# The experts of a decoder layer: square and scaling of finished rows later in full blocks, two low parts earlier, the gather ahead of the store

## The reference

```python
def run_block(args):
    xb, e = args
    h = jax.nn.silu(xb @ w_gate[e]) * (xb @ w_up[e])
    return h @ w_down[e]

ys = lax.map(run_block, (xs, block_expert)).reshape(P, D)
out = jnp.zeros((T + 1, D), jnp.float32).at[slot_tok].add(ys.astype(jnp.float32) * slot_gate[:, None])[:T]
```

## Time and profile before

| | us |
|---|---|
| median of three runs | 2077.36 (2075.55 to 2087.81) |
| the profiled execution | 2084.54 |
| its span, first to last instruction | 2082.6 |
| PE busy in the span | 1935.8 (93%) |
| DVE busy | 1344.3 (65%) |
| ACT busy | 1166.8 (56%) |
| POOL busy | 868.4 (42%) |

### The profile page before, as it was taken

The page is one execution under the profiler, slowest core; times in us unless marked ns, Lnnn a source line. Parts: engine busy times, 40 slices in busy tenths (PEclk is TensorE's granted clock), DMA queues, the critical chain, the costliest instruction groups (busy, mean ns, idle before and its releaser), DMA issues. The chain is left out here.

```text
span 2082.6 us, 39849 instructions
## 1 busy us (share of the span) xinstructions
PE 1935.8 (93%) x12329; PEld 1646.0 (79%) x12330; DVE 1344.3 (65%) x2479; ACT 1166.8 (56%) x2436; POOL 868.4 (42%) x1044
## 2 busy tenths in 40 slices
PE   7999999979999999989999679899999999999996
PEld 6888888867777787878878568788888888788885
DVE  5333333339888888845656559766777777787764
ACT  4211111128888889853333248666666667686763
POOL 3332222213656644431332335445454345344544
PEclk9999999979999999989999889999999999999998
DMA  7433334375363543224543569968878978987852
GB/s 224 147 122 122 121 121 123 114 187 151 107 189 98 131 112 92 69 72 152 166 167 126 209 197 368 359 219 295 288 267 289 361 243 292 364 300 288 287 196 71
DMA packets 230803, 406.35 MB, mean 195 GB/s; under 512 B 31201, under 2 KB 169057, under 8 KB 206480
## 3 DMA queue, kind: packets, MB, share of 16 engines
q1 hardware_dynamic: 201328, 352.08, 49.7%
q0 software_dynamic: 29376, 53.03, 9.6%
HBM read 345.83 MB, written 111.15 MB: 219 GB/s over the span
## 5 line engine op out<-in xcount | busy, mean ns | idle before, releaser
L747 ACT ACTIVATE prob<-score,nmax 128x512 f32<-128x512 f32 (+3 forms) x464 | 264.4, 580 | 24.7 <-DVE nmax L897 24.1
L65 PE MATMUL proj<-w_in_lo,n1T_hi 128*128 128x512 f32 (+1 forms) x640 | 242.8, 379 | 3.5 <-DVE w_in_lo L250 3.4
L897 DVE TENSOR_REDUCE nmax<-score 128x2 f32<-128x1024 f32 (+3 forms) x232 | 212.5, 920 | 39.9 <-PE score L945 38.4
L66 PE MATMUL proj<-w_in_hi,n1T_lo 128*128 128x512 f32 (+1 forms) x640 | 237.3, 371 | 0.0
L67 PE MATMUL proj<-w_in_hi,n1T_hi 128*128 128x512 f32 (+1 forms) x640 | 237.1, 371 | 0.0
L812 POOL TENSOR_SCALAR prob<-prob,scale,lam 128x512 f32<-128x512 f32 (+3 forms) x168 | 139.1, 840 | 152.7 <-DVE scale L884 143.1
L1774 POOL DMA_INDIRECT acc_scratch<-y,own x47 | 143.9, 3062 | 96.7 <-ACT y L1955 79.7
L269 DVE TENSOR_TENSOR cosx<-proj,rope_sb 128x512 f32<-128x512 f32 (+1 forms) x64 | 37.9, 592 | 213.2 <-PE proj L67 213.2
L1978 DVE TENSOR_TENSOR wd_lo<-raw_pieces,wd_hi 128x1024 fp32r<-128x1024 f32 x128 | 148.2, 1217 | 7.5 <-ACT wd_hi L1962 7.5
L764 ACT COPY aT<-aT_ps 128x512 f32<-128x512 f32 (+3 forms) x232 | 122.6, 528 | 51.0 <-PE aT_ps L962 49.1
L1978 DVE TENSOR_TENSOR wg_lo<-raw_pieces,wg_hi 128x1024 fp32r<-128x1024 f32 x124 | 146.9, 1218 | 5.3 <-ACT wg_hi L1940 3.9
(11 more groups left out here) (305 smaller groups left out, 5532.9 us busy)
## 6 DMA issues: line engine op xcount, KB each, us to landing
raw_pieces<-in_w_down SPq DMA_DIRECT2D x64, 1024.0 KB, 9.7
raw_pieces<-in_w_gate SPq DMA_DIRECT2D x62, 1024.0 KB, 6.4
raw_pieces<-in_w_up SPq DMA_DIRECT2D x62, 1024.0 KB, 7.6
qk_scratch<-qkT SPq DMA_DIRECT2D x94, 256.0 KB, 2.4
xT_sb<-in_xT SPq DMA_DIRECT2D x16, 512.0 KB, 5.1
h<-in_x SPq DMA_DIRECT2D x16, 512.0 KB, 6.3
acc_scratch<-h SPq DMA_DIRECT2D x16, 512.0 KB, 3.0
n_scratch<-n SPq DMA_DIRECT2D x16, 512.0 KB, 5.5
```

The lines of the kernel that those rows point to most:

```text
L65: pe.matmul(out, hi, w_lo, start=first, stop=False)
L66: pe.matmul(out, lo, w_hi, start=False, stop=False)
L747: act.activation(prob[:, n % RING, c, 0:w], score[:, n % BUFS, c, 0:w], ACT.Exp, bias=nmax[:, c, n:n + 1], accum_out=part[:, c, n:n + 1]). ...
L897: dve.tensor_reduce(nmax[:, :, n:n + 1], score[:, n % BUFS, :, 0:w], AX.X, ALU.max, negate=True).then_inc(max_ready, 1)
```

## The change

In full blocks four things move; nothing is added or taken away, and small blocks stay.
- ACT: the square stands behind highs 3 to 5 and the first cast of hT, not behind the Silu.
- DVE: lows 3 and 4 stand between the first half of `hid` and the first split of hT; `final` stands behind the second half of `hid` and low 5, just ahead of the second split of hT.
- POOL: the gather of x stands ahead of the store.
- In the last block, which has no highs, lows and gather ahead, the square stands behind the first cast of hT and `final` behind the second half of `hid`.

```diff
@@ -1838,9 +1838,9 @@
                     add(b)
                     normal_root(b)
                     aim_store(b)
-                    store(b)
                     if replaced:
                         gather_ahead(b)
+                    store(b)
                     move_on(b)
@@ -1943,9 +1943,9 @@
                     act.wait_ge(g_done, b + 1)
                     act.wait_ge(h_turned, b * 2 + 1)
                     act.activation(hid[:, :], g_ps[:, :], ACT.Silu).then_inc(silu_ready, 1)
-                    square(b)
                     highs(3, 4, 5)
                     copy_hT(b, 0)
+                    square(b)
                     highs(6)
                     copy_xT(b + 1)
                     copy_hT(b, 1)
@@ -2033,10 +2033,11 @@
                     lows(0, 1, 2)
                     dve.wait_ge(silu_ready, b + 1)
                     hidden(b, 0)
-                    normalize(b)
+                    lows(3, 4)
                     split_hT(b, 0)
                     hidden(b, 1)
-                    lows(3, 4, 5)
+                    lows(5)
+                    normalize(b)
                     split_hT(b, 1)
                     split_xT(b + 1)
                     lows(6, 7, 8, 9, 10, 11)
```

## The result

The changed kernel took 2094.24 us (median of four, 2092.21 to 2096.87), the kernel before 2076.45 (median of four, 2074.87 to 2087.81): a ratio of 1.0078 with a 95% interval of 1.0049 to 1.0106, slower by 0.8%, inside the 1% that the prediction took as no change. It said 2066 with a range to 2084; both are missed.

A forecast was written before the change was run, and what follows sets the result against it. TensorE sets the pace, its gaps mostly waits for hT. Full blocks -38, small blocks +23 and program end +4 sum to -11: 2073.5 us from the profiled 2084.54, 2066 from the median 2077.36; range 2045 to 2084.

The forecast's parts named there:

- Full blocks, -38: 31 full blocks: TensorE's gaps before the down product close, 18.25 us each, 38 us less in all; ends 25 and 42.
- The floor of 18.12 us: A full block without TensorE's 0.62 us gap: 18.14 us, taken as 18.12 from the several 18.75 us blocks.
- 0.1 ahead: Full block of 1464.96 us: `final` 2.98 us behind the square's start; second split ends at 1480.1, TensorE wants it at 1480.24.
- the limit that I had put at 10.9: Full block: `whole` may come until 10.9 us in, formerly 6.2, without delaying ScalarE's second cast of hT.
- The fetch's place, 2.2 us later: GpSimd, full blocks: fetch of `whole` moves from -2.16 to +0.1 us against the next block's start, 2.2 later.
- The small blocks, +23: 15 small blocks: ScalarE's unmoved square waits for the late `whole`, 23 us more in all; ends 8 and 36.
- The price of a late square: Small blocks: 1 us of the square's wait lengthens the block by 1.1 us at first, then 1.7.
- The end of the program, +4: Last block: square, `final`, store, fetch and last gather come later, all on the path, 4 us more; ends 2 and 5.
- A, the DMA engines set the pace: 16 full blocks behind full ones stop near 18.9 us, the DMA being full; 2076 us in all; chance 0.2.
- B, small blocks over 17 us on average: Late `whole` costs every small block alike, 18.57 us each; 22 us slower, 2099 us; chance 0.12.
- C: Small blocks pay only 8 us, as loads move into idle DMA room; 2051 us; chance 0.25.
- D: Moved parts do nothing since VectorE is full, 17.64 of 18.73 us; counted within the DMA rival, no chance of its own.

The follow-up runs named there:

- the kernel with one low part moved: The kernel before with only low part 5 moved behind the split of xT: ratio 0.9861, and 0.9842 when run again.
- low part 5 moved: The changed kernel with low part 5 behind the split of xT instead of ahead of `final`: ratio 1.0142 to the kernel before.
- the square back: The changed kernel with the square of full blocks back behind the Silu: ratio 1.0088 to the kernel before.
- the store behind it: The changed kernel with the fetch of `whole` ahead of the store in full blocks: ratio 0.9946 to the kernel before.
- the load of pieces 2 and 3 later: The changed kernel with the load of weight pieces 2 and 3 held until low part 5 is done: ratio 1.0124 to the kernel before.
- the exchange alone: The kernel before with only GpSimd's gather of x moved ahead of the store: ratio 1.0067.

## Why the prediction was wrong

**Full blocks, -38 against -32.1.** The mechanism was right: the wait for hT was put near 3 us and is 3.7. The floor of 18.12 us was right within 0.1, since the kernel with one low part moved runs blocks of 18.00 and 18.09. But of the changed kernel's 31 full blocks two take 18.00 and 18.02, twenty 18.31 to 18.35, and nine more. The step that failed is "0.1 ahead": `final` would run at 3.0 us behind the square's start. It ran at 3.29 (1466.13 to 1469.42) and with it the second split ended at 15.35 us into the block, where TensorE wanted it at 15.28 (1470.74 + 0.23); the step from one product to the next took 0.43 instead of 0.23, and the next another 0.33. The cause lies on GpSimd: the root took 1.66 us. The changed kernel shows it within itself. In the two blocks of 18.00 and 18.02 us the root took 0.57 and 0.58; here the one of 1273.82, on GpSimd and VectorE:

```profile
1285.77 0.57 POOL L1792 TENSOR_TENSOR rstd<-var,power 128x1 f32<-128x1 f32 x1
...
1285.78 1.25 DVE L1978 TENSOR_TENSOR wu_lo<-raw_pieces,wu_hi 128x1024 fp32r<-128x1024 f32 x1
1286.95 1.27 DVE L1996 SCALAR_TENSOR_TENSOR final<-whole,rstd,gf_bc 128x1024 f32<-128x1024 f32 x1
1288.33 0.42 DVE L1989 TENSOR_TENSOR hT<-u_ps,hT 128x256 fp32r<-128x256 f32 x1
```

The square starts at 10.44 us into it, as in the pattern block, and the second split ends at 14.93 instead of 15.35. With the root at 0.57 in all blocks, low part 5 moved, the step is 0.23 at that place, too. The nine other blocks, 18.49 to 19.13, are the first and members of runs of three or more; in these eight the square starts at 10.8 to 12.3 us, at or past the limit that I had put at 10.9.

The size of the term is no surer than the profile that it is taken from: the repeated profile of before has the full blocks at 600.6 where the first has 604.1.

**The fetch's place, 2.2 us later against 2.75.** The order of GpSimd's steps was followed rightly and their durations were not. From the means of the kernel before (busy, mean ns of one, idle before):

```profile
L1782 POOL DMA_INDIRECT whole<-acc_scratch,whole_at x47 | 53.9, 1147 | 24.0 <-issue 22.9
...
L1792 POOL TENSOR_TENSOR rstd<-var,power 128x1 f32<-128x1 f32 x48 | 27.8, 579 | 3.8
...
L1845 POOL COPY own<-slots 128x3 int32 (+1 forms) x32 | 11.4, 356 | 8.0 <-POOL whole_at L1812 8.0
```

and of the changed kernel:

```profile
L1782 POOL DMA_INDIRECT whole<-acc_scratch,whole_at x47 | 73.5, 1564 | 11.1 <-issue 8.1
...
L1792 POOL TENSOR_TENSOR rstd<-var,power 128x1 f32<-128x1 f32 x48 | 52.6, 1097 | 3.9
...
L1845 POOL COPY own<-slots 128x3 int32 (+1 forms) x32 | 27.8, 868 | 7.9 <-POOL whole_at L1812 7.9
```

The same small instructions, moved beside VectorE's low parts, take 1.9 (root), 2.4 (row numbers) and 1.4 times as long (issue of the fetch) on average, and the first two stand ahead of the fetch.

**The small blocks, +23 against +39.7, the term that failed.** It lies outside its own end of 36. By the kinds of the prediction:

| | before | after | difference | forecast |
|---|---|---|---|---|
| four behind two or more full, early fetch | 56.5 | 81.0 | +24.5 | +12.5 |
| four with a late add | 69.7 | 76.4 | +6.6 | +6 |
| seven behind a single full block | 96.5 | 105.1 | +8.6 | +5 |

Three quarters of the miss is in the first row, and three of its four blocks (20.02, 20.96 and 21.77 us) stand behind runs of three and four full blocks. There the step "in a full block the landing is then at +10.0, under the 10.9 limit: hidden" failed. In the block of 1599.97 the fetch comes at 0.60 and not 0.1, its landing takes 10.5 and not 9.9, and the square starts at 11.1. The landing goes past the limit, so the square, the root, the store and the fetch of that block are late as well, the next fetch goes from 0.6 to 1.75 us behind the start, and y waits for its row numbers (the wait of y for `own`, 26.8 us in 31, before 3.1 in 5). I had treated each block by itself, with a fixed place of the fetch. The lateness is carried from block to block until a block has room. In these eight blocks (first two rows) the landing from issue to square is 10.7 us, where I kept 9.9 (it was 9.7 before): another 0.8. The price of a late square was near enough at 10.35 us (18.3 us of block), too high beyond: 20.0 for a square at 12.4 and 21.8 for one at 13.7, some 1.05 us of block for 1 us and not 1.7. A block with the square at 10.6 whose granted clock stayed at 1.00 took 16.97, so the square's place alone doesn't give the price. What I had wrong is the square's place.

**The end of the program, +4 against +3.0.** Right. The square stands at 10.6 us in the last block, as expected (10.5).

**The rivals.** A, the DMA engines set the pace: refuted as put. Full blocks of 18.00 and 18.09 us run with a DMA share of 1.01 to 1.02 and 376 and 385 GB/s. Little room is left, though: with one low part moved ScalarE waits for raw pieces, 4.4 us in 8 waits in the first profile and 0.9 in the second, where before and changed kernel have no such wait. The figure of some 358 GB/s for one core in the Trainium skill ("DMA: Bandwidth & Descriptors", Specifications), given there as half of what two cores share, is exceeded by 395 GB/s in the block of 1310.83 us, where one core works. B, small blocks over 17 us on average, was nearest: they are at 262.45 / 15 = 17.5. It was put as every block at 18.57 and deciding from 34 us, and it is the mechanism that came. I gave it 0.12, because the landings behind single full blocks were short; that holds (seven blocks at 15.0 us), but the eight others stand at 19.7. C and D fell.

**The scale.** On the profiled executions the sum gave 2073.5 and 2092.2 came: 5.9 from the full blocks, 16.7 from the small ones, less 1.0 at the end and 3.0 from stages that nothing touched. The rest of the distance on the medians (2066 to 2094.24) is that I took 7 us off for the first profile of before, and that the profile after lay 2 below its median. The 7 us were a correction to a median of three; beside the medians of the later comparisons the first profile, 2084.54, was an ordinary one.

## What to carry to other kernels

If one engine waits at one point, first try the smallest move that closes that gap: here one low part moved behind the split gave 1.4 to 1.6%, while the change, which made room by delaying the square and `final` and put the gather of x ahead of the store, delayed a chain (square, root, store, fetch, landing, next square) that comes round once per block. A chain that comes round has to be followed through several blocks in a row, through the block with the least room; a delay that a single block hides adds up in a run of three. And a block kind that the change doesn't edit can pay for it.

## What the runs showed of the hardware

**GpSimd beside VectorE.** The root on 128 x 1 elements takes 0.57 us alone and 1.66 beside a low part of 1.22 us, whose operands both lie in SBUF (1467.63 and 1467.64 in the pattern block). In two blocks with 0.01 or 0.02 us between them it is the other way: root 0.57, low part 1.25 (1285.77 and 1285.78). The copy of row numbers goes from 0.19 (in the last block, which has no low parts) to 0.89. The Trainium skill ("SBUF — State Buffer", Who interferes with whom) states that a VectorE instruction with two SBUF inputs contends with a GpSimd instruction that reads SBUF; the trace agrees, and the kernel with low part 5 moved shows the root at 0.57 us again, in all 31 full blocks. The issues of indirect DMAs are lengthened too (1.02 to between 1.83 and 2.02 us) in such stretches; which part of an issue is held was not tried.

**The landing of an indirect gather.** The same gather of `whole` took 8.8 to 11.2 us from issue to square in small blocks behind two or more full ones, averaged per kernel. It was shortest with the square back and with the store behind it (8.8 both), and longest with the load of pieces 2 and 3 later (11.2). The length of the full blocks ahead does not order it: with the exchange alone they are the longest of these (612.8) and the landing is 10.4. I have no rule that gives it from the trace, and it stays open.
